# The first two doubling levels of a blocked triangular inverse, moved from 128-wide tiles to 32-wide and 64-wide diagonal tiles of TensorE

## What is computed

```
def step(S, inp):
    r_t, w_t, k_t, v_t, kk_t, a_t = inp
    sa = jnp.einsum('bhij,bhj->bhi', S, -kk_t)
    S = (S * w_t[:, :, None, :]
         + sa[..., None] * (kk_t * a_t)[:, :, None, :]
         + v_t[..., None] * k_t[:, :, None, :])
    y = jnp.einsum('bhij,bhj->bhi', S, r_t)
    return S, y
...
_, ys = lax.scan(step, S0, (tmajor(rh), tmajor(wh), tmajor(kh), tmajor(vh), tmajor(kk), tmajor(ah)))
```

## Time and profile before

| | us |
|---|---|
| median of 3 runs | 1515.61 (1515.29 to 1517.06) |
| the profiled execution, its own time | 1515.54 |
| its span in the profile | 1513.5 |
| TensorE busy | 1483.1 (98%) |
| VectorE busy | 1240.9 (82%) |
| ScalarE busy | 1009.2 (67%) |

### The profile page before, as it was taken

One profiled execution on the slowest core, in us unless ns is written; L12 is line 12 of the kernel. 1 busy time (PEld: TensorE's weight loads), 2 busy tenths in 40 slices (PEclk: granted clock), 3 DMA queues, 4 the chain that ended last, 5 costly groups with the idle time before them and its releaser, 6 DMA issues.

```text
span 1513.5 us, 21521 instructions
## 1 busy us (share of the span) xinstructions
PE 1483.1 (98%) x7832; PEld 1238.6 (82%) x7832; DVE 1240.9 (82%) x1367; ACT 1009.2 (67%) x1157; POOL 21.9 (1%) x19
## 2 busy tenths in 40 slices
PE   7999999999899999999999999999999999999997
PEld 5888888799799678888888888888888888888885
DVE  3756666787865279999999999999999999999997
ACT  3544444663523158888888888888878888888886
POOL 0000000000000020000000000000000000000200
PEclk9999999999999999999999999999999999999998
DMA  9889453035404589999999999999999999999990
GB/s 361 322 276 299 168 167 112 1 132 201 140 2 169 181 296 332 397 390 397 395 391 397 395 370 386 395 362 382 393 383 363 393 386 363 395 382 363 349 374 28
DMA packets 206694, 453.54 MB, mean 300 GB/s; under 512 B 8881, under 2 KB 46257, under 8 KB 206386
## 3 DMA queue, kind: packets, MB, share of 16 engines
q1 hardware_dynamic: 203154, 446.12, 80.1%
q0 software_dynamic: 1280, 4.20, 1.0%
q10 hardware_dynamic: 2208, 2.50, 0.5%
HBM read 437.58 MB, written 23.60 MB: 305 GB/s over the span
## 4 chain that ended last, share of the span: by engine, by line
PE 92%; DVE 5%; ACT 2%; DMA 1%; issue 0%; DVEq 0%; ACTq 0%
PE psum L1582 20%; PE psum L1584 20%; PE psum L1583 20%; PE psum L2392 5%; PE psum L2395 3%; PE psum L897 2%; PE psum L2316 2%; PE psum L2356 2%; PE psum L2357 2%; PE psum L2358 2%; PE psum L600 2%; PE psum L1600 2%; PE psum L2309 1%; PE psum L791 1%; PE psum L781 1%; PE psum L696 1%
## 5 line engine op out<-in xcount | busy, mean ns | idle before, releaser
L1790 DVE TENSOR_TENSOR w_lo<-ring,w_hi 128x1024 fp32r<-128x1024 f32 x672 | 810.8, 1224 | 63.3 <-ACT w_hi L1684 15.8
L1684 ACT ACTIVATE w_hi<-ring 128x1024 fp32r<-128x1024 f32 x672 | 711.2, 1062 | 172.7 <-PE psum L1584 172.6
L1582 PE MATMUL psum<-w_hi,xg_split 128*128 128x512 f32 x896 | 353.9, 395 | 0.3 <-DVE xg_split L1881 0.3
L1584 PE MATMUL psum<-w_lo,xg_split 128*128 128x512 f32 x896 | 349.8, 390 | 0.0
L1583 PE MATMUL psum<-w_hi,xg_split 128*128 128x512 f32 x896 | 349.1, 390 | 0.0
L1584 PEld LDWEIGHTS psum<-w_lo,xg_split 128*128 128x128 f32 x896 | 168.3, 188 | 35.5
L1582 PEld LDWEIGHTS psum<-w_hi,xg_split 128*128 128x128 f32 x896 | 168.4, 188 | 34.0 <-DVE xg_split L1881 0.6
L1583 PEld LDWEIGHTS psum<-w_hi,xg_split 128*128 128x128 f32 x896 | 168.6, 188 | 33.5
L1582 PE MATMUL psum<-w_hi,ht_split 128*128 128x512 f32 x448 | 176.2, 393 | 0.0
L1584 PE MATMUL psum<-w_lo,ht_split 128*128 128x512 f32 x448 | 174.7, 390 | 0.0
L1583 PE MATMUL psum<-w_hi,ht_split 128*128 128x512 f32 x448 | 174.5, 390 | 0.0
(11 more groups left out here) (370 smaller groups left out, 1509.0 us busy)
## 6 DMA issues: line engine op xcount, KB each, us to landing
ring<-o_moe_wg_dram SPq DMA_DIRECT2D x56, 2048.0 KB, 10.7
ring<-o_moe_wu_dram SPq DMA_DIRECT2D x56, 2048.0 KB, 11.2
ring<-o_moe_wd_dram SPq DMA_DIRECT2D x56, 2048.0 KB, 11.3
ring<-e_ffn_wg_dram SPq DMA_DIRECT2D x11, 1024.0 KB, 5.5
ring<-e_ffn_wu_dram SPq DMA_DIRECT2D x11, 1024.0 KB, 8.2
ring<-e_ffn_wd_dram SPq DMA_DIRECT2D x11, 1024.0 KB, 11.3
expert_rows<-work SPq DMA_DIRECT2D x1, 8192.0 KB, 27.8
ring<-e_w_in_dram SPq DMA_DIRECT2D x2, 2048.0 KB, 18.4
```

What stands on the lines that cost most here:

```text
L1582: nc.tensor.matmul(dst, x_hi, hi, start=first, stop=False)
L1584: return nc.tensor.matmul(dst, x_hi, lo, start=False, stop=last_)
L1684: nc.scalar.activation(w_hi[:, (4 * i + n) % 4, :], piece(i, n), ACT.Copy).then_inc(m_hi, 1)
L1790: V.tensor_tensor(w_lo[:, r, :], piece(i, n), w_hi[:, r, :].bitcast(F32), ALU.subtract).then_inc(m_lo, 1)
```

## The change

A new constant `quad` (eight columns) says for each 32-row quarter whether a row belongs to it, once for its first 16 rows only and once for all 32.

**Level v = 0** no longer works on the spread tiles. It works on the packed 16x16 inverses `XTc` in three steps of 64 small matmuls each (two pairs, eight heads, four quarters of the array): `blocks_turned` transposes each even block by a matmul with a 16x16 piece of the identity, `blocks_Y` multiplies a 16-row, 32-column piece of A by it, `blocks_X` multiplies a 32x32 tile by the packed odd block. Each of them has 16 moving columns, and the four quarters of one head lie on the four diagonal 32x32 tiles of the array. ScalarE copies and masks between them, in place of VectorE. VectorE writes the even halves of XT from the packed blocks (`spread_even`, two instructions) and the odd halves from the product (`spread_odd`, two).

**Level v = 1** keeps the 128x128 transposes; `level_Y` and `level_X` become two matmuls per head with 64x64 stationary tiles and 32 moving columns on the two diagonal quarters, and VectorE's addition becomes two 64-row instructions per pair.

**Order.** `packed` is cut in two; on VectorE all 15 steps of `recur(1, ...)` now stand behind chunk 0's level v = 1, and on TensorE the five batches of `block_rows(1, ...)` stand later. The zeroing of Yv goes from ScalarE to GpSimd, with half the size, and the identity part of the packed tile is written by ScalarE at the start of the scan.

The core of the diff:

```diff
+    q4 = s // 32 == np.arange(4)[None, :]
+    put("quad", np.concatenate([q4 & (s % 32 < 16), q4], 1))
...
-        Yv = [ru(6 + v).rearrange("p (g l t) -> p g l t", g=4, l=4) for v in range(2)]
+        block_Yc = ru(6, 512).rearrange("p (m t) -> p m t", m=16)
+        block_Xe = ru(6, 256, 512).rearrange("p (m t) -> p m t", m=16)
+        Yv = [None, ru(7).rearrange("p (g l t) -> p g l t", g=4, l=4)]
...
-                    if v == 0:
-                        pe.wait_ge(x_full, 2 * c + gg // 2 + 1)
-                        if c == 1 and gg == 2:
-                            pe.wait_ge(t_sc, 2)
-                    elif v == 2 and gg >= 2:
+                    if v == 2 and gg >= 2:
...
+            quads = [slice(32 * i, 32 * i + 32) for i in range(4)]
+
+            def blocks_turned(c):
+                pe.wait_ge(rec_done, c + 1)
+                for pair in range(2):
+                    for l in range(8):
+                        for qd in quads:
+                            ev = slice(qd.start, qd.start + B0)
+                            last = nc.tensor.matmul(psum[ev, pair, B0 * l:B0 * l + B0], XTc[c][ev, 8 * pair + l, :],
+                                                    ident[ev, ev], start=True, stop=True)
+                    last.then_inc(l_tr, 1)
+
+            def blocks_Y(c):
+                for pair in range(2):
+                    pe.wait_ge(l_xe, turned_at(c, 0, pair))
+                    if c == 1:
+                        pe.wait_ge(t_yc, pair + 1)
+                    for gg, l, k, o, at in heads_of(pair):
+                        n = at // HD
+                        for qd in quads:
+                            ev = slice(qd.start, qd.start + B0)
+                            last = nc.tensor.matmul(psum[qd, 2 + pair, B0 * n:B0 * n + B0], A_all[c][ev, gg, l, 0, qd],
+                                                    block_Xe[ev, 8 * pair + n, :], start=True, stop=True)
+                    last.then_inc(l_y, 1)
+
+            def blocks_X(c, pair):
+                pe.wait_ge(l_yd, masked_at(c, 0, pair))
+                if c == 1:
+                    pe.wait_ge(t_sc, 2)
+                for n in range(8):
+                    for qd in quads:
+                        last = nc.tensor.matmul(psum[qd, 4 + pair, B0 * n:B0 * n + B0], block_Yc[qd, 8 * pair + n, :],
+                                                XTc[c][qd, 8 * pair + n, :], start=True, stop=True)
+                last.then_inc(l_xu, 1)
+
             def level_Y(c, v):
                 for pair in range(2):
                     pe.wait_ge(l_xe, turned_at(c, v, 2 * pair + 1))
-                    if v == 0 and c == 1:
-                        pe.wait_ge(t_yc, pair + 1)
                     for gg, l, k, o, at in heads_of(pair):
-                        last = nc.tensor.matmul(psum[:, 2 + pair, at:at + HD], A_all[c][:, gg, l, 0, :], Xv[v][:, gg, l, :],
-                                                start=True, stop=True)
+                        for i in range(2):
+                            hs, n = slice(HD * i, HD * i + HD), slice(32 * i, 32 * i + 32)
+                            last = nc.tensor.matmul(psum[hs, 2 + pair, at + 32 * i:at + 32 * i + 32], A_all[c][hs, gg, l, 0, hs],
+                                                    Xv[v][hs, gg, l, n], start=True, stop=True)
                     last.then_inc(l_y, 1)
 
             def level_X(c, v, pair):
@@ -788,7 +823,10 @@
                     pe.wait_ge(l_xe, turned_at(c, v, 3))
                 for gg, l, k, o, at in heads_of(pair):
                     odd = XT[c][:, gg, l, :].rearrange("p (b h t) -> p b h t", h=2, t=B0 << v)[:, :, 1, :]
-                    last = nc.tensor.matmul(psum[:, 4 + pair, at:at + HD], Yv[v][:, gg, l, :], odd, start=True, stop=True)
+                    for i in range(2):
+                        hs = slice(HD * i, HD * i + HD)
+                        last = nc.tensor.matmul(psum[hs, 4 + pair, at + 32 * i:at + 32 * i + 32], Yv[v][hs, gg, l, hs],
+                                                odd[hs, i, :], start=True, stop=True)
                 last.then_inc(l_xu, 1)
 
...
-            turned(0, 0)
-            level_Y(0, 0)
+            blocks_turned(0)
+            blocks_Y(0)
+            blocks_X(0, 0)
+            blocks_X(0, 1)
+            turned(0, 1)
+            level_Y(0, 1)
             pe.wait_ge(s_comp, 2)
             pe.wait_ge(s_part, B0 - 1)
             block_rows(1, 0)
             block_rows(1, 1)
-            level_X(0, 0, 0)
-            level_X(0, 0, 1)
-            turned(0, 1)
-            level_Y(0, 1)
-            block_rows(1, 2)
             level_X(0, 1, 0)
             level_X(0, 1, 1)
-            block_rows(1, 3)
             turned(0, 2)
             right_side(0, 0)
+            block_rows(1, 2)
             pe.wait_ge(y_zero, 3)
             top_Y(0)
+            right_side(0, 1)
+            block_rows(1, 3)
+            top_X(0)
             block_rows(1, 4)
-            right_side(0, 1)
-            top_X(0)
             pe.wait_ge(rec_done, 2)
             solved(0)
             outputs(0)
 
-            turned(1, 0)
+            blocks_turned(1)
             pe.wait_ge(t_yc, 2)
             gn_mean(0, 6)
-            level_Y(1, 0)
-            level_X(1, 0, 0)
-            level_X(1, 0, 1)
+            blocks_Y(1)
+            blocks_X(1, 0)
+            blocks_X(1, 1)
             turned(1, 1)
...
+            def blocks_turned(c):
+                for pair in range(2):
+                    act.wait_ge(l_tr, turned_at(c, 0, pair))
+                    nc.scalar.activation(block_Xe[:, 8 * pair:8 * pair + 8, :], r3(psum[:, pair, 0:P], 8), ACT.Copy,
+                                         scale=C("par")[:, 0:1]).then_inc(l_xe, 1)
+
+            def blocks_Y(c):
+                for pair in range(2):
+                    act.wait_ge(l_y, lev(c, 0, pair))
+                    nc.scalar.activation(block_Yc[:, 8 * pair:8 * pair + 8, 0:B0], r3(psum[:, 2 + pair, 0:P], 8), ACT.Copy,
+                                         scale=C("par")[:, 1:2]).then_inc(l_yd, 1)
...
+            nc.scalar.activation(block_Yc[:, :, B0:2 * B0], C("eye16").unsqueeze(1).to_broadcast([P, 16, B0]), ACT.Copy,
+                                 scale=C("par")[:, 1:2]).then_inc(y_zero, 1)
...
-            for v in range(2):
-                nc.scalar.activation(r3(ru(6 + v), U // P), ident.unsqueeze(1).to_broadcast([P, U // P, P]), ACT.Copy,
-                                     scale=0.0).then_inc(y_zero, 1)
-            turned(0, 0)
+            blocks_turned(0)
+            blocks_Y(0)
             turned(0, 1)
             turned(0, 2)
             right_side(0, 0)
...
-            def spread(c):
+            def halves(c, pair):
+
+                return XT[c][:, 2 * pair:2 * pair + 2, :, :].rearrange("p g l (b h t) -> p (g l) b h t", h=2, t=B0)
+
+            def quad(o):
+
+                return C("quad")[:, o:o + 4].unsqueeze(1).unsqueeze(3).to_broadcast([P, 8, 4, B0])
+
+            def spread_even(c):
                 dve.wait_ge(rec_done, c + 1)
-                for gg in range(4):
-                    last = V.tensor_tensor(XT[c][:, gg, :, :].rearrange("p l (b t) -> p l b t", t=B0),
-                                           XTc[c][:, 4 * gg:4 * gg + 4, :].unsqueeze(2).to_broadcast([P, 4, 8, B0]),
-                                           C("blk16").rearrange("p (b t) -> p b t", t=B0).unsqueeze(1).to_broadcast([P, 4, 8, B0]),
-                                           ALU.mult)
-                    if gg % 2 == 1:
-                        last.then_inc(x_full, 1)
+                for pair in range(2):
+                    V.tensor_tensor(halves(c, pair)[:, :, :, 0, :],
+                                    XTc[c][:, 8 * pair:8 * pair + 8, :].unsqueeze(2).to_broadcast([P, 8, 4, B0]), quad(0), ALU.mult)
+
+            def spread_odd(c, pair):
+                dve.wait_ge(l_xu, lev(c, 0, pair))
+                V.tensor_tensor(halves(c, pair)[:, :, :, 1, :],
+                                r3(psum[:, 4 + pair, 0:P], 8).unsqueeze(2).to_broadcast([P, 8, 4, B0]), quad(4),
+                                ALU.mult).then_inc(l_xd, 1)
 
             def level_Y(c, v, pair):
                 w = B0 << v
@@ -1307,8 +1374,12 @@
             def level_X(c, v, pair):
                 w = B0 << v
                 dve.wait_ge(l_xu, lev(c, v, pair))
-                odd = XT[c][:, 2 * pair:2 * pair + 2, :, :].rearrange("p g l (b h t) -> p (g l b) h t", h=2, t=w)[:, :, 1, :]
-                V.tensor_tensor(odd, odd, r3(psum[:, 4 + pair, :], 512 // w), ALU.add).then_inc(l_xd, 1)
+                odd = XT[c][:, 2 * pair:2 * pair + 2, :, :].rearrange("p g l (b h t) -> p (g l) b h t", h=2, t=w)[:, :, :, 1, :]
+                new = psum[:, 4 + pair, :].rearrange("p (m b t) -> p m b t", m=8, t=w)
+                for i in range(2):
+                    hs = slice(HD * i, HD * i + HD)
```

(44 more changed lines are left out.)

## The result

The changed kernel took 1524.06 us (median of 4, 1523.15 to 1524.56) against 1515.45 of the kernel before on the same chip (1514.97 to 1517.06): a ratio of 1.0048, 95% interval 1.0029 to 1.0066. The forecast was 1504, its range ended at 1516. The profiled execution's span went from 1513.5 to 1521.3 us.

What follows compares the result with a forecast made beforehand. TensorE's own instruction time was taken to bound the scan. Chunk 0's -4.9 us and chunk 1's -6.7 gave -11.6: 1515.54 - 11.6 = 1503.9, thus 1504 us; 8-in-10 range 1500.5 to 1516.

Steps and rivals of the forecast that it cites:

- Instructions come in too slowly: Rival: in TensorE's scan, each of six steps waits 2.5 us for an instruction packet, +7.3 us, 1511; chance 0.15.
- Packets may be asked for far ahead: Argument against the slow-supply rival: instruction packets could be requested early, so TensorE's scan would not wait for them.
- the six steps: Level 0 on blocks, three steps per chunk, each forecast at 128 records x 10 ns = 1.28 us.
- The clock falls: Rival: TensorE's clock drops; at half clock for one chunk's level some 10 us; chance 0.03.
- the prediction's own signs of being wrong: Steps of 3 us or more, granted clock under 1, or short steps with scan ending less than 8 us earlier.
- 10 ns for a small record: Level 0's block steps: four diagonal tiles overlap fully, 40/4 = 10 ns a record; forecast chance 0.55.
- The floor of 24 ns: Rival: small records in level 0's six steps cost 24 ns, 3.07 us a step, +10.7, 1514.6; chance 0.17.
- the rival without overlap: Rival: level 0's tiles don't overlap, 39 ns a record, six steps +22.3 us, 1526; chance 0.10.
- 30 ns for a record of 64 columns: Level v = 1 products on two diagonal tiles: 64 records, 1.9 us in place of 3.52.
- 2.0 us of standing before `solved(0)`: End of chunk 0: TensorE idle 2 us, near 439, waiting on VectorE's last recurrence step; `solved(0)` starts about 441.3.
- Chunk 0: First half of the scan, up to `solved(0)`: forecast -4.9 us, after 9.2 us won and about half given back.
- The forecast's wait of the head sums for ScalarE: Chunk 1: ScalarE's squares end at 461.85, behind `gn_centre`, leaving TensorE's head sums waiting, about 0.6 us idle.

## Why the prediction was wrong, step by step

**The step that failed** is the rival "Instructions come in too slowly". It was named with the right mechanism, given 0.15 and no term in the sum, and priced at 2.5 us a packet by assumption. The queue's line had given 48/36 = 1.35 us a packet, and I took request and arrival together to be under twice that. Measured is one packet in 3.5 to 3.7 us while TensorE waits for them, of which the packet itself moves for 0.9 to 1.4. At 2.5 us the rival still came out ahead of before; with what was measured it doesn't. Standing in the six steps was 0.4 + 2.4 + 1.9 in chunk 0 and 2.8 + 4.8 in chunk 1, 12.2 us against a gain of 11.6. "Packets may be asked for far ahead" and "there is time in the long steps ahead" were wrong too: what stood ready lasted 113 to 242 records, not the 384 of a chunk, and at the stops a packet began to move only when the one ahead of it was in use.

The second step that failed is the clock. The rival "The clock falls" had a chance of 0.03, "some 10 us", and stood outside the sum. The stretches at half clock cost 1.3 us in chunk 0's transposes, 2.1 in chunk 1's transposes and head sums, 3.3 behind chunk 0 and 2.7 at the router, 9.4 together. Stops and clock are of nearly the same size, and without the clock's part the span would by estimate be that of the kernel before or a little less (+7.8 - 9.4 us). Two of the prediction's own signs of being wrong were there: steps of over 3 us with idle time between records, and a granted clock under 1.

The Trainium skill, page "Runtime: NRT & Kernel Launch", section "Instruction fetch mechanics", says that instructions come in blocks of 16 KiB, 256 of them, and that crossing a border is mostly hidden. The size agrees with the trace (128 pairs, 16 KB a packet). Hidden it is in every run here whose records are 31 ns apart or more, none of which has more than 128 records of 31 ns in a row. It is not where more than one or two packets of records 10 ns apart follow one another. I hadn't weighed that section; its "mostly hidden" would have spoken for my forecast.

**Right:**
- 10 ns for a small record: 128 in 1.25 us, all four diagonal tiles at once, in one PSUM bank. The floor of 24 ns and the rival without overlap, 0.27 of the chances, fell. The page "TensorE: Matmul & The Clock Gate" of the Trainium skill, section "Wait — 56ns, not 53.3ns?", has starts never closer than about 25 ns; for records on different tiles this trace disagrees. The packing section that the prediction sets against it, with tiles about 4 ns apart, is on that page too, not on the tiling page; it was the nearer of the two.
- 30 ns for a record of 64 columns: 64 in 1.99 us from the first to the next group's (forecast 1.9).
- The first step at 413.10 (forecast 413.5), and 2.0 us of standing before `solved(0)`, behind VectorE's recurrence.
- VectorE in chunk 0. From level v = 1's product Y to the right side the forecast had 419.9 to 428.5, 8.6 us. Measured are 8.5 (425.66 to 434.19), with VectorE's masks and additions ahead of the last transposes, as forecast.

**Mis-sized or missed:**
- The clock, why it was put at nothing. I had read that it stays at 1.00 where TensorE idles 9%. That was one thin stretch, with idle pieces of 1.1 us at most. The prediction itself put 2 us of standing into the order, and didn't ask what the clock would do there.
- Chunk 0. Level 1's transposes began at 422.39 (4.4 late: 4.6 of stops), and the right side at 434.19, 5.7 behind the forecast 428.5. The 1.3 us between the two are the transposes at half clock, 3.27 us for 1.9.
- Small terms. ScalarE's copies took 0.37 us (forecast 0.31). A change between whole-array work and tiles took about 0.1 us, not 0.17; the forecast counted 11 of them.
- The whole, in spans: forecast 1513.5 - 11.6 = 1501.9, measured 1521.3, 19.4 apart. Stops 12.2 and half clock 9.4 make 21.6, so the other terms of the sum came out some 2 us shorter than forecast, most of it in chunk 1's levels. The forecast's wait of the head sums for ScalarE doesn't show there: the squares ended at 478.0 us, and TensorE came to the head sums at 478.97.

**What stays open.** The stop of 4.76 us in chunk 1 (4.8 to 5.0 in the three other kernels with level 0 on blocks) is twice the others. A load of 4 MB ran until about 472 us, and the trace says where the time goes: the packet began to move 3.7 us after TensorE had begun on the one ahead (468.34 to 472.07) and not 1.1, while the one behind it, with the load gone, began after 1.0 (474.48 to 475.51). In the three other kernels it is 3.8 to 3.9 and then 1.2 to 1.7. So the packet started late beside the load; that the load held it is likely, but no run took the load away.

The clock's other stretches have no experiment of their own. The one over chunk 0's level 0 stood in the profiled executions of all five kernels with stops there, and in none of the six without (1.00 from 413.5 to 459 us). The run with wide work between its small records, which has neither stops nor slow clock, speaks for the stops as its cause, but it also keeps TensorE fuller in between. The slow stretch at the router stood in the profiled executions of both kernels with 64x64 tiles as well, at 530 to 542 us, though not in the kernel before; what calls it is not shown, so its 2.7 us can't be laid to the small tiles. Shorter stretches at half clock stand where TensorE didn't stop for instructions, as at 409.8 to 413.2 in three runs, and at 463.7 to 467.1 in the first run with both levels on 64x64 tiles, whose profiled execution was the slowest of its six.

How much the new order costs by itself, with its 2.0 us of standing ahead of `solved(0)`, is not measured either.

## What to carry to other kernels

Price a run of small matmuls twice, by their time in the array and by their number: here 128 records with their weight loads came in each 3.5 to 3.7 us, 27 to 29 ns a pair, and whatever went faster than that for more than one or two packets (113 to 242 records) stood still until the average was back at that rate. A larger tile can win where the small one loses (64x64 at 31 ns a record won 10 us); so can wide work between short runs of fast records. How close to the supply one can go wasn't tested. Where a new order leaves TensorE standing for 2 us, count a slow clock behind it as well; here filler work in the gap took it away.

## What the runs showed of the hardware

- Float32 matmuls on four diagonal 32x32 tiles, all into one PSUM bank, ran at 10 ns a record: 128 in 1.22 to 1.26 us.
- A pair of changes, from whole-array work to small tiles and back, cost 0.22 us by subtraction.
- In runs of 384 such records TensorE stood 1.5 to 2.4 us at each 128 pairs (at the first border 0.4 to 0.6 or not at all), and 2.2 to 5.0 beside a 4 MB load; 242 records had stood ready behind 22 wide transposes, and 128 passed with no stop.
- A packet of 16 KB, 128 pairs, began to move 1.0 to 1.2 us after TensorE, out of a stop, had begun on the one ahead, and was in use 2.3 to 2.7 us after that; beside the 4 MB load it began to move only after 3.7 to 3.9.
- After 2.0 us of standing, TensorE ran at half the clock from 449.2 to 456.0 us, though it was busy all through; with 16 transposes in the gap, the clock stayed at 1.00.
